# One hybrid pooling, S5 and mixture-of-experts layer on one core: a quarter of an output table moved to GpSimd, the pooled half of the output projection in four pieces, and three row spreads moved into DRAM or merged

## The reference, cut to what matters

```python
hx = modulate(rmsnorm(x, g_mix), x_sh1, x_sc1)     # 256 latent tokens, D = 1024
hc = modulate(rmsnorm(ctx, g_mix), c_sh1, c_sc1)   # 256 context tokens
ux, uc = hx @ w_in, hc @ w_in[:, 512:]
# columns 512.. : S5 scan, 2 directions, 32 groups x 16 channels x 64 complex states,
# latent scans start from the context scan's last state; y = Re(C_f h_f) + Re(C_b h_b) + D*u
ssm_x = gelu(y) * sigmoid(gelu(y) @ w_glu + b_glu)
# columns ..512 : windowed means minus themselves, times w_pool, times s_pool
x = x + x_g1 * (concatenate([pool_x, ssm_x]) @ w_out)
hx2 = modulate(rmsnorm(x, g_ffn), x_sh2, x_sc2)
eidx, gate = route(hx2, w_router, b_router)        # best of 4 groups, then top 2 of its 8 experts
y = sum over the 2 chosen of gate * ((silu(h @ w_gate[e]) * (h @ w_up[e])) @ w_down[e])
out = rmsnorm(x + x_g2 * y, g_final)
```

## Time and profile before

| | |
|---|---|
| median of three runs | 686.17 us (685.89 to 686.75) |
| the profiled execution | 685.61 us, its span 683.8 us |
| PE busy | 596.1 us, 87% |
| DVE busy | 207.4 us, 30% |
| ACT busy | 147.6 us, 22% |
| POOL busy | 35.7 us, 5% |
| moved by DMA | 247.27 MB, mean 362 GB/s |

### The profile page before, as it was taken

The page is one execution under the profiler, slowest core; times in us unless marked ns, Lnnn a source line. Parts: engine busy times, 40 slices in busy tenths (PEclk is TensorE's granted clock), DMA queues, the critical chain, the costliest instruction groups (busy, mean ns, idle before and its releaser), DMA issues.

```text
span 683.8 us, 9370 instructions
## 1 busy us (share of the span) xinstructions
PE 596.1 (87%) x3784; PEld 253.1 (37%) x3784; DVE 207.4 (30%) x432; ACT 147.6 (22%) x235; POOL 35.7 (5%) x84
## 2 busy tenths in 40 slices
PE   1878999869878999789889978988997898899995
PEld 0345463446434334234323423422342342234331
DVE  7987979538663002001000200100020010002003
ACT  7163051022112212110301211130121213011111
POOL 4364000000000000000000000000000000000000
PEclk9999999988979999999989999998999999899999
DMA  8992177899866999999999999999999999998951
GB/s 319 417 391 66 30 260 292 302 372 404 335 256 263 424 422 420 422 422 422 422 422 422 421 422 422 422 422 422 422 422 422 422 422 422 422 422 342 422 230 62
DMA packets 45807, 247.27 MB, mean 362 GB/s; under 512 B 8548, under 2 KB 11252, under 8 KB 18520
## 3 DMA queue, kind: packets, MB, share of 16 engines
q1 hardware_dynamic: 41032, 244.45, 87.9%
q10 hardware_dynamic: 4448, 1.57, 0.9%
q0 software_dynamic: 304, 0.93, 0.4%
HBM read 242.75 MB, written 2.10 MB: 358 GB/s over the span
## 4 chain that ended last, share of the span: by engine, by line
PE 64%; DMA 21%; DVE 3%; issue 2%; ACT 2%; SPq 1%; ACTq 0%; POOL 0%; DVEq 0%; POOLq 0%
DMA wts<-in_w_up 21%; PE ps L784 20%; PE ps L819 16%; PE ps L758 5%; PE ps L540 4%; PE ps L752 4%; PE ps L549 2%; PE ps L617 2%; PE ps L666 1%; PE ps L677 1%; PE ps L795 1%; PE ps L463 1%; DVE ra L1070 1%; PE ps L647 1%; PE ps L566 1%
## 5 line engine op out<-in xcount | busy, mean ns | idle before, releaser
L784 PE MATMUL ps<-wts,ra 128*64 128x512 f32 x512 | 240.1, 624 | 37.3 <-DMA wts<-in_w_up 36.1
L785 PE MATMUL ps<-wts,ra 128*64 128x512 f32 x512 | 240.2, 624 | 0.0
L784 PEld LDWEIGHTS ps<-wts,ra 128*64 128x64 f32 x512 | 70.5, 143 | 186.5 <-issue 137.2
L819 PE MATMUL ps<-rc,ra 128*32 128x512 f32 x512 | 111.4, 593 | 0.0
L819 PE MATMUL ps<-wts,ra 128*32 128x512 f32 x512 | 111.4, 593 | 0.0
L1070 DVE TENSOR_TENSOR ra<-ra,ps 128x256 f32<-128x256 f32 x32 | 13.5, 421 | 297.7 <-ACT ra L1023 297.5
L1017 ACT COPY ra<-ps 128x512 f32<-128x512 f32 x32 | 33.6, 1049 | 232.5 <-PE ps L785 232.5
L785 PEld LDWEIGHTS ps<-wts,ra 128*64 128x64 f32 x512 | 70.5, 143 | 0.0
L819 PEld LDWEIGHTS ps<-wts,ra 128*32 128x32 f32 x512 | 29.1, 110 | 73.2 <-issue 73.2
L1070 DVE TENSOR_TENSOR cb<-ps,ra 128x512 f32<-128x512 f32 x32 | 22.1, 692 | 103.4 <-PE ps L819 103.4
L1012 ACT COPY ra<-ps 128x512 f32<-128x512 f32 x32 | 18.5, 588 | 114.5 <-PE ps L752 108.6
(11 more groups left out here) (228 smaller groups left out, 507.4 us busy)
## 6 DMA issues: line engine op xcount, KB each, us to landing
wts<-in_w_up SPq DMA_DIRECT2D x64, 1024.0 KB, 15.3
wts<-in_w_gate SPq DMA_DIRECT2D x64, 1024.0 KB, 13.2
wts<-in_w_down SPq DMA_DIRECT2D x30, 1024.0 KB, 9.4
rc<-in_w_down SPq DMA_DIRECT2D x30, 1024.0 KB, 12.5
wts<-in_w_mod SPq DMA_DIRECT2D x15, 1024.0 KB, 13.1
r<-in_w_mod SPq DMA_DIRECT2D x7, 1024.0 KB, 7.3
wts<-in_w_in SPq DMA_DIRECT2D x2, 2048.0 KB, 23.0
wts<-in_w_out SPq DMA_DIRECT2D x2, 2048.0 KB, 11.6
```

The costliest lines, as they stand in the source:

```text
L784: pe.matmul(ps[0:64, 4 + b, :], st, Wg[b][:, k, :], start=(k == 0), stop=(k == KD - 1))
L785: mm = pe.matmul(ps[64:128, 4 + b, :], st, Wu[b][:, k, :], start=(k == 0), stop=(k == KD - 1))
L819: mm = pe.matmul(ps[32 * j:32 * j + 32, BANKS[n], :], hid[:, j, f, SLOTS * t:SLOTS * t + SLOTS], Wd[j][:, f, 512 * h:512 * h + 512], start ...
```

## The change

It has these parts. (1) One of the four parts of MO (d = 1, r = 0) is made by GpSimd (POOL): six tensor_tensor instructions of 128 x 1024 with scratch in SBUF, after the last lag kernels and turns; DVE makes the other three and waits for `mo_back` before the scan. (2) The eight turns of SA for d = 1 are put between the matmuls of `u_ssm(1)`; three of ACT's copies for d = 0 go to DVE, between two parts of SA, and ACT's order changes with them. (3) The pooled half of the output projection becomes `mix_pool(0..3)`, of eight matmuls each: before the HP products, behind them, behind the transposes and behind the GLU. (4) The Toeplitz kernels lie in `wts`, not in `ra`, and are loaded before the last two chunks of the second modulation third; w_pool is loaded later. (5) The rows g1 and sh2 are written to DRAM by ACT and read back by one DMA to all partitions (1 MB); the two PE spreads and two ACT copies go. (6) The scale is spread and summed over partitions by four matmuls of 512 columns, and one DVE instruction makes A2b from PSUM and a row of g_ffn that came through DRAM (0.5 MB); L684, the diagonal, L690 and L994 go. (7) The last modulation third gets four buffers, one semaphore a chunk and another place in SP's order, with two sums of eight before the GLU's end rather than three. (8) In each expert pass only `gather(0)` and `gather(1)` stand before `gate_up`; 2 and 3 stand behind the first half of expert j = 0, and each pair of chunks waits for its own `xm_ready`.

```diff
-        TT = ra[:, 4096:8192].rearrange("p (t n) -> p t n", t=L)
-
-        E = wts[:, 4096:4608]
+        TT = wts[:, 4096:8192].rearrange("p (t n) -> p t n", t=L)
+
+        E = wts[:, 20480:20992]
...
             sp.wait_ge(S("s_mm"), 8)
             w_out_v = w_out[0].rearrange("(k p) n -> p k n", p=P)
-            sp.dma_start(wpool, w_pool[0].rearrange("g c d -> c g d")).then_inc(S("wpool_in"), 16)
             sp.dma_start(wo_pool, w_out_v[:, 0:4, :]).then_inc(S("wo_pool_in"), 16)
-            for k in range(6, KD):
-                mod_chunk(1, k)
-
-            sp.wait_ge(S("u_pool_mm"), NT)
-
             sp.wait_ge(S("kt_ready"), 2)
             for t in range(L):
...
+            for k in range(6, KD):
+                mod_chunk(1, k)
+
+            sp.wait_ge(S("u_pool_mm"), NT)
+            sp.dma_start(wpool, w_pool[0].rearrange("g c d -> c g d")).then_inc(S("wpool_in"), 16)
...
             for k in range(3):
                 mod_chunk(2, k)
-
-            for k in range(3, 6):
-                mod_chunk(2, k)
-            sp.wait_ge(S("mix_pool"), 1)
+            sp.wait_ge(S("gff_row"), 16)
+            sp.dma_start(gffb, row_dram[1:2, 0:D].broadcast_to([P, D])).then_inc(S("gff_in"), 16)
+            sp.wait_ge(S("mod1_row"), 16)
+            sp.dma_start(ra[:, 6144:8192], row_dram[0:1].broadcast_to([P, 2048])).then_inc(S("g1_in"), 16)
+            sp.wait_ge(S("pool_mm"), 1)
+            mod_chunk(2, 3)
+
             sp.wait_ge(S("hp_ready"), 1)
+            mod_chunk(2, 4)
             sp.wait_ge(S("y_mm"), 1)
             for t in range(NT):
                 sp.dma_start(x2[:, t, :], x[0, t * P:(t + 1) * P]).then_inc(S(f"xres_in{t}"), 16)
+            mod_chunk(2, 5)
             gu_load(sp, 0, 0, 0, "up")
             gu_load(sp, 0, 0, 1, "up")
-            for k in range(6, KD):
-                mod_chunk(2, k)
+            mod_chunk(2, 6)
             for half in range(2):
-                down_load(sp, lambda j: j, half, (0, 1))
+                down_load(sp, lambda j: j, half, (1,))
+            mod_chunk(2, 7)
+            sp.wait_ge(S("mix_pool"), 1)
+            for half in range(2):
+                down_load(sp, lambda j: j, half, (0,))
...
+            gp.wait_ge(S("kk_mm"), 2)
+            gp.wait_ge(S("sa_t"), 16)
...
+            t = cb[:, 3072:4096].rearrange("p (g s j) -> p g s j", g=8, s=L)
+            for h in range(2):
+                g = slice(8 * h, 8 * h + 8)
...
+                gp.tensor_tensor(MOv[:, 1, 0, g], pr, cr, ALU.mult)
+                step(gp.tensor_tensor(t, pi, ci, ALU.mult))
+                step(gp.tensor_tensor(MOv[:, 1, 0, g], MOv[:, 1, 0, g], t, ALU.subtract))
+            gp.sem_inc(S("mo_back"), 1)
...
-            u_ssm(1)
-            turn_sa(1, 0, range(4))
-            turn_sa(1, 1, range(4))
+            u_ssm(1, itertools.chain(turn_sa(1, 0), turn_sa(1, 1)))
...
-            for n in range(4):
-                for k in range(4):
-                    mm = pe.matmul(ps[:, n, :], cat[:, k, P * (n // 2):P * (n // 2) + P],
-                                   wo_pool[:, k, 512 * (n % 2):512 * (n % 2) + 512], start=(k == 0), stop=False)
-            mm.then_inc(S("mix_pool"), 1)
...
+            mix_pool(0)
 
             pe.wait_ge(S("hp_ready"), 1)
...
-            pe.wait_ge(S("g1_ready"), 1)
-            spread(1, 2, 6)
+            mix_pool(1)
 
             pe.wait_ge(S("ysb_ready"), 1)
...
             mm.then_inc(S("y_t"), 1)
+            mix_pool(2)
...
+            mix_pool(3).then_inc(S("mix_pool"), 1)
             pe.wait_ge(S("wo_ssm_in"), 16)
...
                     pe.wait_ge(S("mod2_used"), KD)
...
+                    for h in range(2):
+                        pe.matmul(ps[:, 6 + h, :], ones, acc[:, 512 * h:512 * h + 512], start=True, stop=False)
+                        mm = pe.matmul(ps[:, 6 + h, :], ones[32 * h:32 * h + 1, :], modrow[32 * h:32 * h + 1, 2, :], start=False, stop=True)
                     mm.then_inc(S("scale_mm"), 1)
...
             gather(0)
             gather(1)
-            gather(2)
             pe.wait_ge(S("passes_ready"), 1)
-            gather(3)
...
+                    if j == 0 and k % 2 == 0:
+                        pe.wait_ge(S("xm_ready"), 4 * i + k // 2 + 1)
...
+                    if j == 0 and k == 3:
+                        pe.wait_ge(S("out_copy"), 4 * i + 4)
+                        gather(2)
+                        gather(3)
...
+            def take_turns():
+
+                for n in (5, 6, 7):
+                    dve.wait_ge(S("sa_t"), n + 1)
+                    dve.tensor_copy(ST[:, 0, 1, 4 * (n % 4):4 * (n % 4) + 4, :],
...
-            powers_times(MOv, PW, CT, 1, -1, "mo_half")
-            dve.wait_ge(S("mo_half"), 4)
+            powers_times(MOv, PW, CT, 1, -1, "mo_half", rs=(1,))
+            dve.wait_ge(S("mo_half"), 3)
+            dve.wait_ge(S("mo_back"), 1)
...
             dve.wait_ge(S("scale_mm"), 1)
-            link(tt(A2, ps[:, 5, 0:KD], vt[:, V_B2:V_B2 + KD], ALU.add))
...
+            dve.wait_ge(S("gff_in"), 16)
+            link(dve.scalar_tensor_tensor(A2b.rearrange("p (k q) -> p k q", k=KD), ps[:, 6:8, :].rearrange("p a (k q) -> p (a k) q", q=P), 1.0,
+                                          gffb.rearrange("p (q k) -> p k q", k=KD), ALU.add, ALU.mult))
```

More of the change, by code:

```diff
@@ L1 @@
+import itertools
 from contextlib import ExitStack
@@ L472, in mod_turn, with st_copies, turn_sa @@
                 mm.then_inc(S("mod_t"), 1)
-            def turn_sa(d, r, part):
+            def st_copies(n):
+                return n + 1 if n < 5 else n - 2
+            def turn_sa(d, r):
                 pe.wait_ge(S("sa_ready"), 2 * d + r + 1)
-                for g4 in part:
+                for g4 in range(4):
                     n = 8 * d + 4 * r + g4
@@ L505, in _ @@
                 if k == 6:
-                    turn_sa(0, 0, range(4))
-                if k == 7:
-                    turn_sa(0, 1, range(2))
+                    for n in turn_sa(0, 0):
+                        pass
                 mod_chunk(0, k, 4)
-            turn_sa(0, 1, range(2, 4))
             mod_turn(0, 4)
-            turn_x(3)
+            for n in turn_sa(0, 1):
+                pass
             def lag_kernels(d):
                 pe.wait_ge(S("cb_ready"), 1)
-                pe.wait_ge(S("st_copy"), (8, 15)[d])
+                if d == 0:
+                    pe.wait_ge(S("st_copy_dve"), 3)
+                else:
+                    pe.wait_ge(S("st_copy"), st_copies(14))
                 for q in range(4):
@@ L531, in turn_kernels, with u_ssm @@
                     mm.then_inc(S("kt_t"), 1)
-            def u_ssm(q):
+            def u_ssm(q, turns=()):
+                turns = iter(turns)
                 if q == 3:
@@ L541, in u_ssm @@
                                    start=(k == 0), stop=(k == KD - 1))
-                    if q == 0 and k < 4:
-                        turn_x(k + 4)
+                    if q == 0 and k < 5:
+                        turn_x(k + 3)
+                    next(turns, None)
                 mm.then_inc(S("u_ssm_mm"), 1)
@@ L627, in _, with mix_pool @@
                               TT[:, :, SG * grp:SG * grp + SG], start=(g < 2), stop=False, skip_group_check=True)
-            def spread(v_r, j0, bank):
-                for h in range(2):
-                    j = j0 + h
-                    mm = pe.matmul(ps[:, bank + h, :], ones[32 * j:32 * j + 1, :], modrow[32 * j:32 * j + 1, v_r, :],
-                                   start=True, stop=True)
-                mm.then_inc(S("spread_mm"), 1)
-            pe.wait_ge(S("modrow"), 2)
-            pe.wait_ge(S("s_ev"), 8)
-            spread(1, 0, 6)
+            def mix_pool(n):
+                for k in range(4):
+                    mm = pe.matmul(ps[:, n, :], cat[:, k, P * (n // 2):P * (n // 2) + P],
+                                   wo_pool[:, k, 512 * (n % 2):512 * (n % 2) + 512], start=(k == 0), stop=False)
+                return mm
+            pe.wait_ge(S("wo_pool_in"), 16)
+            pe.wait_ge(S("cat_pool"), 1)
+            mix_pool(0)
             pe.wait_ge(S("hp_ready"), 1)
@@ L843, in four @@
                     pe.wait_ge(S("slots"), i + 2)
-                    for r in range(4):
+                    for r in range(2):
                         pe.wait_ge(S("out_copy"), 4 * i + 5 + r)
@@ L943, in _ @@
             u_evacuate(0)
+            for n in range(8, 2 * KD):
+                copy_st(n)
             u_evacuate(1)
-            copy_st(1, 0)
-            copy_st(1, 1)
             u_evacuate(2)
@@ L1144, in _, with powers_times @@
             dve.sem_inc(S("bbar_ready"), 1)
-            def powers_times(dst, pw, m, d, sign_im, done):
-                    for rr in range(2):
+            def powers_times(dst, pw, m, d, sign_im, done, rs=(0, 1), between=None):
+                    for rr in rs:
+                        if between and rr == 1:
+                            between()
```

(10 more changed lines are left out.)

139 lines of the change are left out of this document (62 added, 77 removed).

## The result

The changed kernel takes 691.12 us in the median of 18 runs (685.93 to 695.14), the kernel before, run beside it, 686.03 (18 runs): ratio 1.007, 95% interval 1.0047 to 1.0093. The forecast was 677.9 us, with a range of 674 to 684 and 8% for slower. The profiled execution took 688.25 us, its span 686.2; so this one execution lies 2.9 us under its median and 2.6 over the profiled execution of before.

A forecast was written before the change was run, and what follows sets the result against it. The prediction took the expert weight loads as the bound, so an earlier first product brings the end forward: -7.3 - 0.95 + 0.8 - 0.9 = -8.3 us, from 685.6 to 677.3 profiled, median 677.9, range 674 to 684.

The forecast's parts named there:

- PE around it: PE's chain from the pooling half to the SSM half's first two pieces: 156.1 us in place of 164.37, 8.3 earlier.
- Scale: Scale up to the second residual: sums and rows 2.8 us, A2b 1.5; second residual at 175.4 instead of 182.65.
- The cover of 4.4 us: PE's expected wait for HP before the HP products, to hide w_pool and modulation chunks up to 4 us late.
- The gap: Issue gap between the two halves of the HP products, taken as 1.67 us within 5.7 us for the whole.
- rival D: HP ready earlier but PE at half clock over HP products and mix_pool(1): up to 5 us lost, 682.9; chance 0.10.
- the entry: Start of the expert passes: first product needs one ACT copy, not three, gaining 0.95 us, and comes at 204.35.
- The hole at the last pass: Loads missing at 624 to 628 us, put at 2.2 us; split gathers were to change the end by -0.9.
- no wait for the Toeplitz transfers: DVE's 6.2 us wait before HP goes: transfers in by 112 us, asked for at 119, HP ready at 129.1.
- the split projection: Pooled projection's pieces fill PE's waits around the HP products: of its 14 us, 5 to 6 were to be hidden.
- lag kernels 2: Second lag kernels, behind the moved turns: start at 65.3 us in place of 67.77, 2.5 us earlier.
- The table's price: Six POOL products at 2.3 us each, done at 88.5 with DVE's share; scan then starts 1.1 us earlier than before.
- B: POOL's table slower, above 3.65 us a piece, so the scan starts late: 689.3 us at the upper bound; chance 0.07.

The follow-up runs named there:

- run with the chunks first: Changed kernel, with SP issuing modulation chunks 6 and 7 of the second third before the 15 Toeplitz transfers: 691.24 us, 1.0048 of the kernel before.
- run with wo_pool late: The kernel with the gathers as before, with the 2 MB load of wo_pool issued behind w_pool: 682.24 us, 0.9934 of the kernel before the change.
- quiet run: The kernel with the gathers as before, with SP issuing no loads between wo_ssm and the end of the HP products: 694.97 us, one run.
- three pairs: Quarter table back on DVE, against changed kernel (1.0051; 1.007), kernel with the gathers as before (0.9974; 0.9979), run with wo_pool late (0.9929; 0.9934).
- kernel with the gathers as before: Changed kernel with Toeplitz transfers on ACT's queue, expert 1's down loads behind the last modulation chunk, and part 8 undone: 684.71 us, 0.9979 of the kernel before.

## Why the prediction was wrong

**The step that failed** is in PE around it: the later w_pool and modulation chunks, up to 4 us late, cost nothing. They were not up to 4 us late: PE stood 5.57 us for chunk 6 and 0.76 for chunk 7, and had stood for neither before. The forecast costed the move of the Toeplitz transfers for what waits for them, and not for what is queued behind them: 14 us of SP's queue, two issues of it taking 2.77 and 1.73 us where most take 0.6, and DMA engines at 281 GB/s. A sentence under Scale made it worse: the DMA of that time has had its 422 GB/s in hand since 111 us. The idle DMA time was from 112 to 128 us (shares 0.50 and 0.72 before) and the change filled it. With the half clock that came with the standing (chunk 6 took 1.93 us, before 1.04; so chunk 7), PE was done with mix_pool(0) at 135.6 rather than 124.7. Of these 10.9 us, 6.3 are the two waits, 2.8 the half clock over the chunks and the windows behind them, and 1.7 come from the front, where PE was 0.8 us earlier than before and not 2.5. The cover of 4.4 us was real, and 6.5 us went over it. The run with the chunks first shows that the order within the queue only moves the wait; the run with wo_pool late shows that taking 2 MB out of the stretch removes most of it (1.53 us left).

**The sum, term by term**, of what the second residual is later than forecast (8.9 us):
- HP products begin: +6.5, as told.
- HP products: 8.2 us, not 5.7: +2.5. The gap was taken from before at 1.67 us and became 3.73, as full DMA engines stand beside it; the quiet run has 0.94.
- mix_pool(1): 4.8 rather than 3.5 (+1.3), at the lowered clock that PE has behind the gap (0.70 from 144 to 148 us). This is rival D in a small way; up to 5 us were thought possible there.
- Transposes, GLU and the two pieces: 0.8, 2.2 and 0.2 less than forecast. The GLU's 9.1 us of before were in part at half clock (0.50 from 154 to 158 us); at full clock it took 6.9.
- Scale: 4.3 rather than 2.8 (+1.5). A pass of 512 columns was put at 0.35 us; the four pairs took 1.05 each, 0.53 a pass. The rows for this stood in the trace of before: L734 and L735, later in the chain, have the same shapes and took 4.1 us. A2b: 2.26 with its handover rather than 1.7 (+0.5).

**Behind it**: the entry gave 0.1 us more than forecast, but the first half of the pass then took 6.15 us to its reload rather than 3.7 (half clock): +2.4. Together 8.9 - 0.1 + 2.4 = 11.2. From the reload to the end of the span it is 0.6 us less than before, where the forecast had 0.1 (0.8 and -0.9), and 0.25 more lie around the span. That gives the 10.95 by which the forecast for the profiled execution, 677.3, was too low. The hole at the last pass was put at 2.2 us, from one window; it was 3.2 with the next.

**The other 2 to 3 us**, from there to the median, go with the clock. Within the 18 runs of the changed kernel the mean granted clock lies between 0.938 and 0.957 and the time goes with it (correlation -0.85): the three runs at 0.952 and over took 685.9 to 686.7 us. The median clock is 0.944; the kernel before had 0.953 to 0.955 in the runs beside the experiments, and the kernel with wo_pool late 0.958. PE stood longer and more often, and behind its long stands (5.57 and 3.26 us) it started again at 1.2 GHz. The forecast priced the standing and not the restart, except once, as D. That the restarts make up the difference of the medians is argued, not shown. Where the runs at low clock lose their time was not seen in the changed kernel itself, of which only one execution has a trace; the run with the chunks first (691.44 us in profile) shows one such case, 4 us at the scale.

**What was right.** Scan at 88.74 (forecast 88.5), HP ready at 129.3 (129.1), no wait for the Toeplitz transfers, the split projection, the entry's single copy, the direction at the last pass. The scan's time was right for a wrong reason, though: lag kernels 2 began only 0.97 us earlier, not 2.5, and u_ssm and the state inputs then set 88.74 by themselves, where the forecast had them ready at 87.1 and POOL as the last. That the two came out alike is luck. The table's price was off as well (2.85 us a piece on average for 2.3, with DVE slowed by it), but it did not matter, as three pairs show. The Trainium skill, GPSIMD Engine Reference, section Performance versus the Vector engine, advises VectorE for elementwise work; by this rule the quarter would have stayed on DVE, and the three pairs agree: it gained nothing.

**Rivals.** B would have ended on the slower side by POOL being late; DVE never waited for POOL. The slower outcome had another mechanism, one that the working had met and dismissed in a clause. The kernel with wo_pool late took 682.2 us, still 4.3 over the forecast; its profiled execution, also 682.2, is 4.9 over the 677.3. Its second residual stands at 179.26, 3.9 late: 3.4 in the HP products with their gap and 0.5 in mix_pool(1), 1.3 for the last modulation sum, 1.5 at the scale and 0.5 at A2b, less 3.3 that GLU, transposes and the rest took under their price. Another 1.4 lie before the first product, where it does without the 0.95 of part 8, and 0.3 come back behind it.

## What to carry to other kernels

When a set of transfers is moved ahead in a queue, list what is issued behind it and where each of those is waited for, and check the DMA engines' share in the very window into which it moves: a mean over the stage, or the room of a later window, says nothing. Small transfers can cost the others more than their bytes, and an order that delays large loads not needed until later is the cheap remedy (2 MB moved by 16 us here were worth 0.45%). Price a stall of PE with its restart at the lower clock, and try a part of a change without its most intricate piece: the GpSimd table added a hand-over between two engines and no time.

## What was not expected of the hardware

- Fifteen transfers of 32 to 256 KB, from SBUF to SBUF, held the DMA engines, with the loads among them, at share 1.0 and 252 to 311 GB/s from 104 to 116 us, where loads from HBM alone moved 422. In the kernel with the gathers as before they have ACT's queue (q10) almost to themselves: from 92 to 150 us it moved 2.11 MB and took 12.6% of the time of the 16 engines. That is 7.3 us of all engines for 2.1 MB, where the loads of SP's queue in the same stretch (19.50 MB, 89.4%) would take 5.6 for as many bytes: most of the price is the bytes themselves.
- A run of 256 matmuls of 64 x 128 that takes 3.8 us undisturbed got a gap of 3.4 to 3.8 us with 410 to 426 GB/s beside it (2.05 in one trace where the products ahead of it ran slower), 0.94 with idle DMA engines and a short piece of work ahead, and none with idle DMA engines and a long piece ahead.
- A two-input product of 128 x 1024 on POOL took 1.92 to 3.23 us, and stretched DVE's, beside it, from 1.22 to as much as 3.40: two engines made together what one makes alone in the same time.
